# Three gathers in flight instead of five in a product-key retrieval kernel

## The chip, the cores and the metric

The kernel runs on one core of one Trainium2 chip. The metric is the device time of one execution in microseconds; the number quoted for a kernel is the median of several runs. Beside the timed runs there is one profiled execution, from which every view below comes. All arithmetic is 32-bit, on TensorE (PE), VectorE (DVE), ScalarE (ACT) and GpSimd (POOL); SyncE (SP) and ACT issue the direct DMA loads, and POOL issues the indirect ones, which are called gathers here.

## The reference

The input is 256 tokens of width 1024. There are two layers. Each has a mixer (dilated attention and pooling in layer 0, a gated unit in layer 1) and then a channel mixer with product-key retrieval, which is where the change lies:

```python
q = (ht @ w_q).reshape(T, PEER_HEADS, 2, PEER_HALF_DIM)
scores = jnp.einsum('thic,hikc->thik', q, sub_keys)
sv, si = lax.top_k(scores, PEER_TOPK)               # 16 of 128, twice per head
cand = sv[:, :, 0, :, None] + sv[:, :, 1, None, :]
best, ci = lax.top_k(cand.reshape(T, PEER_HEADS, -1), PEER_TOPK)
expert = i1 * PEER_N_KEYS + i2                      # 128 experts per token, of 16384
gate = jax.nn.softmax(best, axis=-1)
hid = jax.nn.gelu(jnp.einsum('cd,ckd->ck', xb, w_down[eb]))
out = jnp.einsum('ck,ckd->cd', gb * hid, w_up[eb])
```

The two expert tables hold 16384 rows of 1024 numbers for each layer.

## The kernel before, in words

**Two ways to the same sum.** The last 160 tokens (DENSE) are handled densely: all 16384 rows of the down table are multiplied with them on TensorE, in 128 blocks of 512 KB, the results are gated with a matrix that is zero where an expert was not picked, and 128 blocks of the up table are multiplied in turn. The first 96 tokens are handled sparsely: their own 128 experts are gathered from memory. One gather brings 128 rows of 4 KB, 512 KB in all, one row to each partition. 96 gathers (ROWS) from the down table serve the 96 tokens of a layer, and 96 more from the up table. For each gathered row VectorE takes one dot product (line 1501, function `dots`, called from `early_dot` in the find stage), or one multiply-add for the up table (line 1618).

**The stages of a layer's channel mixer**, in order of time (layer 0; layer 1 in brackets):

- *The find stage*, about 160 to 337 us (912 to 1092 us). PE multiplies down blocks 0 to 76. Meanwhile DVE finds the picks of tokens 0 to 127 (lines 1466 to 1473 and 1554), after which their gathers can start, then those of tokens 128 to 255. Between the pieces of the second half DVE takes 40 dot products of gathered rows (EARLY = 40), and only then writes the gates of the second half (line 1568). PE must wait for those before it transposes them (lines 1211 and 1214) and goes on with block 77.
- *The one-hot stage*, about 347 to 474 us (1096 to 1225 us). It has 40 passes. In each, PE multiplies one down block and then one set of one-hot matrices (the rows `ps<-oh_buf,ret`). The one-hot matrices of a pass are written half by POOL (two instructions of line 584, function `build_first`), half by DVE and ACT. They have two buffers, so POOL may be two passes ahead of PE.
- *The up stage*, about 474 to 770 us (1223 to 1520 us): 128 up blocks on PE, 96 gathers of the up table.

**What sets the order around the change.** POOL runs its instructions in the order in which they are written. First it issues the first 49 down gathers (`asked = EARLY + RING - 1`). Then, from the fourth of its 40 passes on, it builds the one-hots of a pass and issues the gathers for which a place in the ring will be free. Its gathers write a ring of 10 row buffers of 512 KB. A gather waits for the dot product that last read its buffer (`row_used`), and, if it is a down gather, also for the landing of an earlier gather:

```python
if IN_FLIGHT <= q < ROWS:                                   # line 558
    slot, filled, _ = uses[q - IN_FLIGHT + l * GATHERS]
    pool.wait_ge(row_full[slot], 16 * (filled + 1))
```

While POOL waits there, everything after it on POOL waits as well. The up gathers (q from 96 on) have no such wait.

Down blocks are loaded into 8 buffers, each when PE has used up the block 8 before it. SP issues all of them up to block 39 and from block 80 on; between those SP issues the even ones and ACT the odd ones. Before it issues block 40, SP waits for the gates of the first 128 tokens (line 492).

Of the kernel before, what the change touches and what calls it, by code (L numbers as in the profile page):

```python
# [57 lines left out]
PARTS = P // MORE  # L58
PICKS = RH * TOPK // 2
EXPERTS = KEYS * KEYS  # L60
RING, IN_FLIGHT = 10, 5
UP_RING = 8
DOWN_RAW = 8
ROWS = PICKS + MORE
# [1679 lines left out]
```

## Time and profile before

| | us |
|---|---|
| median of 3 runs (1534.59 to 1537.02) | 1535.36 |
| the profiled execution's own time | 1542.12 |
| its span, first to last instruction | 1540.3 |
| PE busy | 1493.3 (97%) |
| DVE busy | 887.1 (58%) |
| ACT busy | 476.6 (31%) |
| POOL busy | 721.3 (47%) |
| POOL waiting at line 568 for the landing of a down gather | 87.5, 49 times |
| DVE waiting at line 1501 for a gathered row | 24.3, 15 times |

PE is nearly always busy; what it waits for is short and sits between stages. The page's row of GB/s gives the DMA traffic in 40 slices of 38.5 us; it stands near 409 over most of the up stages. "Busy" on POOL at line 568 is the time to write the descriptors of a gather (about 1 us), not the transfer. An idle time in brackets names what ended it.

### The profile page before, as it was taken

The numbers are of one execution on the slowest core, as the hardware profiler recorded it, in microseconds if no ns is written. First come the engines' busy times: TensorE is split into PE (matmuls) and PEld (weight loads), VectorE is DVE, ScalarE is ACT, GpSimd is POOL, SyncE is SP. The second block draws the span as 40 slices with busy tenths as digits, with TensorE's granted clock in tenths as the row PEclk, the third lists the DMA queues.
The fourth block names the chain that finished last, engine by engine and source line by source line (L and its number), as shares of the span: only waits on it lengthen the run. The fifth ranks groups of instructions, "written<-read, shape, count | busy, mean of one in ns | idle before, by whom it ended". The sixth has DMA issues, their size and how long they took to land.

```text
span 1540.3 us, 29722 instructions
## 1 busy us (share of the span) xinstructions
PE 1493.3 (97%) x10668; PEld 1449.4 (94%) x10668; DVE 887.1 (58%) x2900; ACT 476.6 (31%) x1199; POOL 721.3 (47%) x632
## 2 busy tenths in 40 slices
PE   7999999999999999999999999989999999999996
PEld 5789999999999999999977899989999999999996
DVE  1631889856886344443723339998388843444473
ACT  4663331227882000000046542211588600000001
POOL 5568023338996223323457741333599832233250
PEclk9999999999999999999999999999999999999999
DMA  7344899998999999999944468999999999999993
GB/s 276 131 137 165 282 357 406 408 402 314 382 387 392 409 409 410 409 410 410 384 164 161 155 217 301 407 403 409 350 374 378 384 409 409 410 409 410 410 409 135
DMA packets 144992, 523.12 MB, mean 340 GB/s; under 512 B 17008, under 2 KB 17264, under 8 KB 144496
## 3 DMA queue, kind: packets, MB, share of 16 engines
q1 hardware_dynamic: 67696, 240.62, 41.6%
q0 software_dynamic: 55296, 201.35, 33.4%
q10 hardware_dynamic: 21888, 79.70, 13.0%
q8 instruction: 65, 1.06, 0.3%
q14 instruction: 47, 0.39, 0.1%
HBM read 519.48 MB, written 1.05 MB: 338 GB/s over the span
## 4 chain that ended last, share of the span: by engine, by line
PE 78%; DVE 8%; DMA 7%; ACT 3%; issue 2%; POOL 1%; SPq 0%; another core or an unknown queue 0%; DVEq 0%; POOLq 0%; ACTq 0%
PE ps L937 77%; DMA arena<-in_rows,ret 4%; DVE arena L1554 2%; DMA spare<-in_wu 1%; DVE arena L1501 1%; DMA raw<-in_wd 1%; DVE oh_buf L1469 1%; POOL w_lo L551 1%; DVE oh_buf L1466 1%; DVE arena L1473 1%; ACT arena L626 1%; DMA raw<-in_wm 1%; PE ps L945 1%; ACT hT_hi L653 1%; ACT w_hi L638 1%
## 5 line engine op out<-in xcount | busy, mean ns | idle before, releaser
L937 PE MATMUL ps<-arena,raw 128*128 128x160 f32 (+1 forms) x2944 | 416.7, 301 | 4.6 <-DMA raw<-in_wd 4.4
L937 PE MATMUL ps<-arena,w_raw 128*128 128x160 f32 (+1 forms) x2944 | 414.9, 299 | 2.8 <-issue 2.8
L937 PEld LDWEIGHTS ps<-arena,raw 128*128 128x128 f32 x2944 | 407.1, 192 | 6.3 <-DMA raw<-in_wd 4.6
L937 PEld LDWEIGHTS ps<-arena,w_raw 128*128 128x128 f32 x2944 | 403.5, 190 | 4.6 <-issue 4.5
L568 POOL DMA_INDIRECT arena<-in_wu,ret x192 | 190.7, 993 | 362.8 <-DVE oh_buf L1618 272.2
L568 POOL DMA_INDIRECT arena<-in_rows,ret x192 | 202.7, 1056 | 298.3 <-ACT ret L826 104.5
L1618 DVE SCALAR_TENSOR_TENSOR oh_buf<-arena,ret,oh_buf 128x1024 f32<-128x1024 f32 x126 | 161.8, 1284 | 239.1 <-DMA arena<-in_wu,ret 238.9
L551 POOL TENSOR_TENSOR w_lo<-raw,w_hi 128x1024 fp32r<-128x1024 f32 x80 | 193.3, 2424 | 100.7 <-PE ps L937 67.9
L1501 DVE SCALAR_TENSOR_TENSOR arena<-arena,ps 128x1024 f32<-128x1024 f32 x128 | 153.7, 1213 | 0.0
L916 ACT ACTIVATE arena<-ident 128x768 f32<-128x768 f32 x2 | 1.7, 842 | 448.4 <-PE ps L937 448.4
L584 POOL TENSOR_SCALAR oh_buf<-iota,ret 128x128 f32<-128x128 f32 x160 | 127.2, 803 | 15.4 <-PE ps L937 11.3
L804 ACT ACTIVATE arena<-ps 128x160 f32<-128x160 f32 x160 | 48.5, 303 | 276.6 <-PE ps L937 267.0
L937 PE MATMUL ps<-arena 128*128 (+5 forms) x824 | 115.8, 306 | 2.9 <-issue 1.5
L1618 DVE SCALAR_TENSOR_TENSOR ret<-arena,ret 128x1024 f32<-128x1024 f32 x62 | 84.1, 1356 | 57.2 <-DMA arena<-in_wu,ret 54.5
L937 PEld LDWEIGHTS ps<-arena 128*128 128x128 f32 (+2 forms) x824 | 109.7, 190 | 5.8 <-issue 2.5
L638 ACT ACTIVATE w_hi<-raw 128x1024 fp32r<-128x1024 f32 x80 | 83.7, 1060 | 75.6 <-DMA raw<-in_wm 50.6
L849 ACT ACTIVATE ret<-iota,ret 128x128 f32<-128x128 f32 x320 | 100.8, 386 | 4.6 <-PE ps L937 4.6
L1554 DVE SCALAR_TENSOR_TENSOR arena<-iota,ret,ps 128x54 f32<-128x54 f32 x512 | 100.7, 266 | 2.0 <-issue 1.6
L1501 DVE SCALAR_TENSOR_TENSOR arena<-arena,spare 128x1024 f32<-128x1024 f32 x64 | 77.0, 1221 | 24.3 <-DMA arena<-in_rows,ret 24.3
L937 PE MATMUL ps<-arena,spare 128*128 (+1 forms) x576 | 86.6, 300 | 3.4 <-DMA spare<-in_wu 3.3
L937 PE MATMUL ps<-oh_buf,ret 128*128 128x128 f32 x640 | 85.5, 277 | 2.9 <-issue 2.7
L1599 DVE TENSOR_TENSOR arena<-arena,ps 128x512 f32<-128x512 f32 x80 | 54.9, 686 | 56.1 <-PE ps L937 48.6
(144 smaller groups left out, 1779.4 us busy)
## 6 DMA issues: line engine op xcount, KB each, us to landing
raw<-in_wd SPq DMA_DIRECT2D x108, 512.0 KB
w_raw<-in_wd SPq DMA_DIRECT2D x108, 512.0 KB
raw<-in_wm SPq DMA_DIRECT2D x80, 512.0 KB
raw<-in_wu ACTq DMA_DIRECT2D x28, 512.0 KB
raw<-in_wu SPq DMA_DIRECT2D x28, 512.0 KB
w_raw<-in_wu SPq DMA_DIRECT2D x28, 512.0 KB
w_raw<-in_wu ACTq DMA_DIRECT2D x28, 512.0 KB
low_rows<-in_wu SPq DMA_DIRECT2D x22, 512.0 KB
```

The costliest lines, as they stand in the source:

```text
L551: nc.gpsimd.tensor_tensor(w_lo[:, s % WLO, :], raw[:, s, :], whs[:, s].bitcast(F32), ALU.subtract).then_inc(wlo_pool, 1)
L568: nc.gpsimd.indirect_dma_start(ring[s], None, table, bass.IndirectOffsetOnAxis(ap=index, axis=0)).then_inc(row_full[s], 16)
L584: nc.gpsimd.tensor_scalar(oh1g[:, g % 2, k, :], iota[:, :], i1T[:, t:t + 1], gT[:, t:t + 1], ALU.is_equal, ALU.mult).then_inc(oh1_pool, 1)
L626: nc.scalar.activation(junk[:, t, ks], src[:, t, ks], ACT.Square, accum_out=sumsq[:, k, t:t + 1]).then_inc(sumsq_done, 1)
L638: nc.scalar.activation(whs[:, s], raw[:, s, :], ACT.Copy).then_inc(whi_done, 1)
L804: nc.scalar.activation(block_of(b), down_psum(b % SLOTS), ACT.Gelu_apprx_tanh).then_inc(h_done, 1)
L849: nc.scalar.activation(oh2[:, g % 2, k, :], iota[:, :], ACT.Abs, scale=-1.0, bias=i2T[:, t:t + 1]).then_inc(oh2_far, 1)
L937: return nc.tensor.matmul(out, lhsT, rhs, start=start, stop=stop, skip_group_check=shared)
L1501: nc.vector.scalar_tensor_tensor(row, row, 1.0, more_rows if more else h_rows, ALU.mult, ALU.mult, accum_out=(more_hid if more else row_hi ...
L1554: step(nc.vector.scalar_tensor_tensor(found[:, (j * 8 + k) % 24, :], places, cif[:, t, n:n + 1], pay[:, h, :], ALU.is_equal, ALU.mult, acc ...
L1599: nc.vector.tensor_tensor(part, part, gates, ALU.mult).then_inc(gmul_done, 1)
L1618: ins = nc.vector.scalar_tensor_tensor(out, row, coef[:, j:j + 1], out, ALU.mult, ALU.add)
```

## The change

A gather of the down table waits for the landing of the third one before it, in place of the fifth.

```diff
-RING, IN_FLIGHT = 10, 5
+RING, IN_FLIGHT = 10, 3
```

IN_FLIGHT is used only in `gather` (lines 558 and 559). The ring still has 10 buffers, and POOL still asks for as many gathers at each point of its program. No instruction is added, removed or moved on any engine: only the value of 93 waits in each layer is another. The first three gathers of a layer have no such wait now, as the first five had none before.

## Rows read from the trace of the kernel before

**Rows 1.** The page: GB/s in 40 slices; the gathers' queue, packets, MB, share
```profile
GB/s 276 131 137 165 282 357 406 408 402 314 382 387 392 409 409 410 409 410 410 384 164 161 155 217 301 407 403 409 350 374 378 384 409 409 410 409 410 410 409 135
...
q0 software_dynamic: 55296, 201.35, 33.4%
```
**Rows 2.** Chain of waits, layer 0's find stage: start us, us, what
```profile
268.76 16.64 DMA arena<-in_rows,ret
...
319.37 16.29 DMA arena<-in_rows,ret
```
**Rows 3.** PE's timeline: start us, us, engine, line, operation, count [idle before <-releaser]
```profile
308.17 8.86 PE L937 MATMUL ps<-arena,raw 128*128 128x160 f32 x64
...
337.74 0.44 PE L1211 MATMUL ps<-ident,ret 128*128 128x128 f32 x2 [1.15 <-DVE ret L1568]
...
1009.45 11.72 PE L937 MATMUL ps<-arena,raw 128*128 128x160 f32 x64 [4.40 <-DMA raw<-in_wd]
```
**Rows 4.** POOL's timeline, find stages of layer 0 and layer 1
```profile
272.30 0.94 POOL L568 DMA_INDIRECT arena<-in_rows,ret  x1 [2.60 <-DMA arena<-in_rows,ret]
...
334.10 1.30 POOL L568 DMA_INDIRECT arena<-in_rows,ret  x1 [1.73 <-DMA arena<-in_rows,ret]
...
957.17 0.98 POOL L568 DMA_INDIRECT arena<-in_rows,ret  x1 [52.50 <-ACT ret L826]
...
964.36 0.94 POOL L568 DMA_INDIRECT arena<-in_rows,ret  x1 [1.22 <-DMA arena<-in_rows,ret]
...
971.83 0.94 POOL L568 DMA_INDIRECT arena<-in_rows,ret  x1 [1.30 <-DMA arena<-in_rows,ret]
```
**Rows 5.** Busy us of the engines by stretch, granted clock, DMA share, GB/s
```profile
269.00:308.00 39.00, 39.00 (x289) 39.00 (x288) 34.71 (x204) 8.35 (x21) 15.54 (x12) 1.00 1.03 408
385.00:424.00 39.00, 39.00 (x307) 39.00 (x307) 33.79 (x70) 33.21 (x103) 35.43 (x41) 1.00 0.99 381
1010.00:1050.00 40.00, 40.00 (x278) 40.00 (x277) 39.88 (x239) 8.04 (x20) 16.08 (x14) 0.94 1.02 404
```
**Rows 6.** Waits of layer 1, 1060 to 1100 us: us, times, longest
```profile
DVE ret L1572 <- PE ps L1214: 9.1, 1, 9.1
```
**Rows 7.** Chain of waits, layer 1's find stage
```profile
991.15 18.25 DMA raw<-in_wd
```
**Rows 8.** POOL's timeline, layer 0's one-hot stage
```profile
369.24 1.03 POOL L568 DMA_INDIRECT arena<-in_rows,ret  x1 [0.17 <-DVE arena L1501]
370.57 0.94 POOL L568 DMA_INDIRECT arena<-in_rows,ret  x1 [0.30 <-issue]
...
373.31 1.03 POOL L568 DMA_INDIRECT arena<-in_rows,ret  x1 [0.17 <-issue]
...
376.14 1.03 POOL L568 DMA_INDIRECT arena<-in_rows,ret  x1 [0.17 <-issue]
...
378.97 1.03 POOL L568 DMA_INDIRECT arena<-in_rows,ret  x1 [0.16 <-issue]
...
381.80 1.03 POOL L568 DMA_INDIRECT arena<-in_rows,ret  x1 [0.17 <-issue]
383.13 0.94 POOL L568 DMA_INDIRECT arena<-in_rows,ret  x1 [0.30 <-issue]
...
436.12 1.03 POOL L568 DMA_INDIRECT arena<-in_rows,ret  x1 [0.17 <-issue]
...
448.67 1.03 POOL L568 DMA_INDIRECT arena<-in_rows,ret  x1 [0.17 <-DMA arena<-in_rows,ret]
...
463.54 1.59 POOL L584 TENSOR_SCALAR oh_buf<-iota,ret 128x128 f32<-128x128 f32 x2
...
469.20 1.59 POOL L584 TENSOR_SCALAR oh_buf<-iota,ret 128x128 f32<-128x128 f32 x2
```
**Rows 9.** PE's timeline, layer 0's one-hot stage
```profile
465.23 1.13 PE L937 MATMUL ps<-oh_buf,ret 128*128 128x128 f32 x8 [0.29 <-issue]
...
471.44 1.05 PE L937 MATMUL ps<-oh_buf,ret 128*128 128x128 f32 x8
```

## The prediction, made before the changed kernel ran

> **What bounds the kernel now.** I read the page's slices first, then the chain of waits, then the timelines of PE, POOL and DVE at the two places where the chain leaves PE. PE is busy 97% of the span, so a change that adds no work to PE can only act through PE's waits. The slices say that DMA is the second limit. It stands at 406 to 410 GB/s where down blocks and gathers run together, and at 381 to 392 in the middle of the one-hot stages [rows 1]. A gather is 201.35 MB over 384 gathers, 0.524 MB [rows 1], so at 408 GB/s any 512 KB piece, gather or block, costs 1.28 us of all the DMA there is.
>
> The chain leaves PE in layer 0's find stage. From 268.76 to 335.68 us it runs through four landings of gathered rows, about 16 us each, then DVE's last dot products and the gates, and PE waits 1.15 us for these [rows 2, 3]. So layer 0's find stage ends when the 40th row has landed. Layer 1's does not: there DVE has its gates ready and waits 9.1 us for PE [rows 6]. PE itself was late there, because a down block took 18.25 us to land [rows 7]. PE stood for 4.40 us, and the next 64 rows of matmuls took 11.72 us where 64 take 8.86 otherwise [rows 3]; the granted clock over that stretch is 0.94 [rows 5]. That stall therefore cost 4.4 + 2.9 = 7.3 us.
>
> In the one-hot stage PE is busy without a break, but so is POOL. POOL finishes a pass's two one-hots at 463.54 + 1.59 = 465.13, and PE's product of them starts at 465.23 after 0.29 us of idling [rows 8, 9]: PE was waiting for POOL there, whatever name the view gives to the gap. The last pass is ready at 470.79 and used at 471.44, so POOL ends the stage with 0.65 us in hand [rows 8, 9]. A wait put into POOL here is a stall of PE, nearly one for one.
>
> **The one-hot stage, step by step.** 47 down gathers are issued between POOL's passes. The wait for the fifth gather ahead is met nearly always: the idle time before them is a bare 0.16 to 0.30 us [rows 8]. What counts now is the distance to the third one ahead. From the issue times 369.24, 370.57, 373.31, 376.14, 378.97, 381.80, 383.13 [rows 8] the distances are 6.90, 8.40, 8.49 and 6.99 us, and the pattern repeats about every 5 gathers. If a gather lands in less than 6.9 us from its issue, nothing changes. How long does one take? The shortest that the trace shows is the first gather of layer 1, issued at 957.17 and landed before the sixth could start at 964.36: 7.0 us or a little more [rows 4], with others close behind it. The longest inside the stage is the one issued at 436.12, which released the gather at 448.67: 12.4 us [rows 8]. That was with up to five outstanding; with three less queues ahead, and the load at 381 GB/s is below the 408 of the full engine [rows 5]. I take 7.6 us, near the short row. Then each group of five has to be stretched by 7.6 - 6.9 = 0.7 us (one stretch serves the three tight distances, since each spans it), and 47 / 5 = 9.4 groups give 6.6 us, less about 0.6 that POOL has in hand: 6 us for each layer, 12 in all. The ends: 0 below 6.9 us. At 9 us the loose distances tighten as well; every three gathers then take 9 us, so 47 take 141 us, where five take 383.13 - 370.57 = 12.56 us now, and 47 take 118: 23 us in each layer. DVE and ACT have the same buffers to fill and are not the ones late.
>
> **Layer 0's find stage.** From 272.30 to 334.10, over 19 gathers, POOL issued one every 61.8 / 19 = 3.25 us, mostly on the landing of the fifth ahead [rows 4], and each took some 16.3 us [rows 2], which is 5 x 3.27. PE used four down blocks (64 matmul rows) in 8.86 us [rows 3], one every 2.2 us. In GB/s that is 161 for gathers and 237 for blocks, together the 408 of the stretch [rows 5] within 3%. So gathers get what is left by the blocks. With three in flight DMA should stay full, and the time between landings stays 3.25 us, at 9.8 us each. But if the engines serve the two kinds in proportion to what is outstanding, 5 gathers at 161 stand against 7.4 blocks at 237, and 3 gathers against 4.4. Three more blocks have then landed at any moment, and three fewer gathers, though PE has no use for the blocks. The 40th row is late by those three: 3 x 1.28 = 3.9 us if PE's stall leaves all DMA to them, 3 x 3.25 = 9.8 us if not. I take 5 us. A stall of that length brought 2.9 us of slower clock in layer 1, so 8 us. The ends are 0 (DMA does not care how many are outstanding) and 13.
>
> The Trainium skill speaks against this term. Its page "DMA: Bandwidth & Descriptors", section "Queues, rings and completion order", says that each DMA engine takes turns between the queues that have work, a packet at a time. By that rule the share of the gathers would not depend on how many are outstanding so long as there are some, and this term would be 0. The trace doesn't decide it.
>
> **Layer 1's find stage.** Fewer gathers ahead of the late block should shorten its 18.25 us: two of 0.524 MB are 2.6 us, and the 4.4 us stall with its clock loss could go altogether, up to 7.3 us gained. DVE's lead of 9.1 us [rows 6] is larger than that. But the same lateness of the rows as in layer 0, 4 to 10 us, eats the lead: PE comes 7.3 us earlier and finds the gates 9.1 - 4 = 5 us early or 9.1 - 10 = 1 us late. I take 0 for the sum of the two, with ends -7 and +6.
>
> **The up stage.** Its gathers have no such wait, its DMA stands at 409 GB/s [rows 1] and its length is not touched. What the down stages lose is not given back, since only 16 buffers of up blocks can be filled ahead.
>
> **The sum.** 8 + 0 + 12 = 20 us. The profiled execution took 1542.12 us, span 1540.3, and would take 1562; its own time is 6.8 us above the median of the runs. The median of 1535.4 goes to 1555 us.
>
> **The rivals.**
>
> *Queues take turns.* The depth does not change any share of the DMA. Then layer 0's find stage costs 0, layer 1 gains some of its stall, say 4 us, and the one-hot stage still pays 12: 1535.4 + 8 = 1543 us. For it: in layer 0 gathers got exactly what blocks left over, which turn-taking explains as well. Against it: at the start of layer 1's gathers the sixth to the tenth were issued on four landings between 964.36 and 971.83 [rows 4], one in 1.87 us or 280 GB/s, more than an even turn with the blocks would give.
>
> *Blocks come first, and the gathers land soon enough.* The mechanism is the late block of layer 1, and the price is its stall with the clock, 7.3 us. It decides if a gather lands in under 6.9 us in the one-hot stage, so that POOL never waits, and if the 40th row of layer 0 is less than 1 us later. Then the kernel is at 1535.4 - 6 = 1529 us. For it: three in flight should cut the latency, and the rule about turns supports the rest. Against it: 7.0 us is the shortest landing in the rows, already above 6.9.
>
> *POOL pays in full.* The landing stays at 9 us in the one-hot stage because down blocks of both queues and the gathers keep the engines at 0.99 busy [rows 5]. 23 x 2 + 8 = 54 us: 1589 us. For it: the 12.4 us row. Against it: with POOL slower the load falls, and the latency with it.
>
> *Nothing happens.* The landing is at the edge, gain and loss cancel: 1535 us. POOL's 49 waits for a landing just get another name.
>
> **How the numbers follow.** The forecast of about 1555 has 0.45, turns 0.20, POOL in full 0.12, blocks first 0.14, nothing 0.09. Changes under 0.2% (3 us) can't be told from none for this kernel. Slower: 0.45 + 0.20 + 0.12, less a little for the edge of the second, 0.76. Faster: 0.15. Same: 0.09. The range has to reach from the faster case's upper edge, 1531, to beyond the likeliest one's high side (8 us of landing, 10 us in each layer, and 13 in the find stage: 1569) and close to POOL in full: 1531 to 1588. The likeliest case alone spans 1543 to 1570.
>
> **What would show it.** In the one-hot stage, line 568 of POOL should show waits for landings of 0.3 to 1 us at about three of five gathers, and PE should show gaps at the products from oh_buf, summing to some 6 us in each layer. In layer 0's find stage PE's wait at line 1211 should be 4 to 10 us in place of 1.15, with the landings near 10 us and a gather every 3.3 us. In layer 1 the stall at 1009 us should be shorter and DVE's 9.1 us wait should shrink. The forecast is wrong if the one-hot stages keep their length, which would mean that landings take under 6.9 us, or if gathers come further apart than 3.3 us in the find stage, which would mean that three do not keep DMA full.

## The result, and where the time went

The changed kernel takes 1576.53 us (median of 4, 1574.87 to 1578.53) against 1536.19 us for the kernel before in the same comparison. The ratio is 1.0247, with a 95% interval of 1.023 to 1.0263: about 38 us, or 2.5%, slower (the medians are 40 us apart). The forecast was 20 us. The measured time lies inside the stated range, but the loss is twice the forecast.

The change also adds two waits to each layer, for the fourth and the fifth gather; the other 91 have another value.

The two profiled executions are 1542.12 and 1574.87 us, 32.7 us apart. The one of before took longer than any of the timed runs and the one of after is the fastest of its own, so the stages below add up to 32.7 and not to 38.

The page's slices answer to those of [rows 1], and the group of POOL's gathers shows the new waits:

```profile
GB/s 278 121 148 183 289 360 407 381 355 332 361 351 371 409 409 410 410 410 409 346 194 155 159 221 333 406 397 402 266 350 348 334 407 408 409 410 409 410 409 139
...
L568 POOL DMA_INDIRECT arena<-in_rows,ret x192 | 201.7, 1051 | 341.9 <-DMA arena<-in_rows,ret 186.9
```

Slices 8 to 13 of the 40 stand at 332 to 381 where they stood at 314 to 408, and the up stages at 409 to 410 as before. POOL waits 186.9 us for landings of down gathers where it waited 87.5.

PE's timeline in the changed kernel (start us, us, engine, line, operation, idle before and what ended it) answers to [rows 3, 9]:

```profile
342.32 0.69 PE L1211 MATMUL ps<-ident,ret 128*128 128x128 f32 x2 [9.94 <-DVE ret L1568]
355.12 1.13 PE L937 MATMUL ps<-oh_buf,ret 128*128 128x128 f32 x8 [1.07 <-ACT ret L857]
...
483.48 1.05 PE L937 MATMUL ps<-oh_buf,ret 128*128 128x128 f32 x8
...
1106.02 0.69 PE L1211 MATMUL ps<-ident,ret 128*128 128x128 f32 x2 [9.95 <-DVE ret L1568]
1106.92 9.08 PE L937 MATMUL ps<-arena,w_raw 128*128 128x160 f32 x48
...
1121.85 1.87 PE L937 MATMUL ps<-oh_buf,ret 128*128 128x128 f32 x8 [3.67 <-issue]
...
1223.10 1.13 PE L937 MATMUL ps<-oh_buf,ret 128*128 128x128 f32 x8 [1.85 <-ACT ret L857]
...
1254.62 1.05 PE L937 MATMUL ps<-oh_buf,ret 128*128 128x128 f32 x8
```

PE waits almost 10 us for the gates in both layers. In layer 1 the stall on a late down block is gone (no idle of PE between 990 and 1096 us). These starts, with the first gather of each layer (205.00 and 957.17 us before, 204.35 and 968.88 after), cut the span into stages. "Find" runs from a layer's first gather to PE's row of line 1211, "handover" from there to PE's first product of one-hots, "one-hot" from that product to the last one.

| stage | before | after | more |
|---|---|---|---|
| to the first gather, layer 0 | 205.00 | 204.35 | -0.65 |
| find, layer 0 | 132.74 | 137.97 | 5.23 |
| handover, layer 0 | 11.52 | 12.80 | 1.28 |
| one-hot, layer 0 | 122.18 | 128.36 | 6.18 |
| up stage, and layer 1 to its first gather | 485.73 | 485.40 | -0.33 |
| find, layer 1 | 135.55 | 137.14 | 1.59 |
| handover, layer 1 | 9.14 | 15.83 | 6.69 |
| one-hot, layer 1 | 120.45 | 132.77 | 12.32 |
| the rest | 317.99 | 318.38 | 0.39 |

The sum is 32.7 us. The one-hot stages have 18.5 of it, the find stages with their handovers 14.8, and the up stages have neither paid nor won. The kernel with the seventh gather ahead (experiment 4) takes the same time as before, and its profiled execution (1537.09 us) is nearer to the median. Against that one the same cuts give 37.7 us: 20.9 in the one-hot stages, 7.0 in find and handover of layer 0, 9.8 in those of layer 1. The layer 1 starts of before come from its own timeline:

```profile
1092.72 0.38 PE L1211 MATMUL ps<-ident,ret 128*128 128x128 f32 x2
...
1101.86 1.05 PE L937 MATMUL ps<-oh_buf,ret 128*128 128x128 f32 x8
...
1222.31 1.05 PE L937 MATMUL ps<-oh_buf,ret 128*128 128x128 f32 x8
```

In the one-hot stage POOL's timeline of the changed kernel (layer 1) answers to [rows 8]:

```profile
1173.44 1.03 POOL L568 DMA_INDIRECT arena<-in_rows,ret  x1 [0.17 <-DMA arena<-in_rows,ret]
...
1176.27 1.03 POOL L568 DMA_INDIRECT arena<-in_rows,ret  x1 [0.17 <-issue]
...
1179.10 1.03 POOL L568 DMA_INDIRECT arena<-in_rows,ret  x1 [0.17 <-issue]
1182.01 0.94 POOL L568 DMA_INDIRECT arena<-in_rows,ret  x1 [1.88 <-DMA arena<-in_rows,ret]
1182.99 1.59 POOL L584 TENSOR_SCALAR oh_buf<-iota,ret 128x128 f32<-128x128 f32 x2
...
1187.57 1.03 POOL L568 DMA_INDIRECT arena<-in_rows,ret  x1 [0.17 <-DMA arena<-in_rows,ret]
...
1196.34 0.94 POOL L568 DMA_INDIRECT arena<-in_rows,ret  x1 [2.08 <-DMA arena<-in_rows,ret]
```

Where a gather waits, it is the second of a pass with two. In all, 5 gathers of layer 0's one-hot stage and 7 of layer 1's wait longer than 0.3 us, 7.6 and 11.9 us together, and PE stands for 6.5 and 8.3 us. The third ahead was issued at 1173.44 and releases it at 1182.01, 8.6 us later; the next time it is 8.8 us (1187.57 to 1196.34). Over all such waits of this kernel and of experiment 2 it is 7.8 to 9.8 us, mostly 8 to 9. The idle time is 1.88 and 2.08 us, POOL's one-hots of the next pass come later by that, and PE shows a gap of some 1.8 us, as at 1223.10, once the lead is spent.

### The profile page after: what moved, and what is told of

Read it like the earlier page. It is cut to its first block, busy times and chain, and to the rows that moved or that the text cites. A ratio compares the mean times of both kernels' runs of the same rounds, so it can differ in the third digit from the quotient of the medians.

```text
span 1573.0 us, 29724 instructions
## 1 busy us (share of the span) xinstructions
PE 1497.2 (95%) x10668; PEld 1452.7 (92%) x10668; DVE 887.8 (56%) x2900; ACT 478.1 (30%) x1199; POOL 716.9 (46%) x632
## 3 DMA queue, kind: packets, MB, share of 16 engines
HBM read 519.48 MB, written 1.05 MB: 331 GB/s over the span
## 4 chain that ended last, share of the span: by engine, by line
PE 50%; DMA 30%; DVE 9%; issue 5%; ACT 4%; POOL 2%; SPq 0%; DVEq 0%; POOLq 0%; ACTq 0%
PE ps L937 49%; DMA arena<-in_wu,ret 15%; DMA arena<-in_rows,ret 14%; DVE arena L1554 2%; DVE ret L1618 1%; POOL w_lo L551 1%; DVE arena L1501 1%; DVE oh_buf L1469 1%; DMA spare<-in_wu 1%; ACT arena L626 1%; PE ps L945 1%; DVE oh_buf L1466 1%; DMA raw<-in_wm 1%; ACT hT_hi L653 1%; DVE oh_buf L1618 1%
## 5 line engine op out<-in xcount | busy, mean ns | idle before, releaser
L937 PEld LDWEIGHTS ps<-arena,w_raw 128*128 128x128 f32 x2944 | 409.3, 192 | 0.0
L568 POOL DMA_INDIRECT arena<-in_rows,ret x192 | 201.7, 1051 | 341.9 <-DMA arena<-in_rows,ret 186.9
L568 POOL DMA_INDIRECT arena<-in_wu,ret x192 | 187.5, 976 | 364.3 <-DVE oh_buf L1618 280.9
L638 ACT ACTIVATE w_hi<-raw 128x1024 fp32r<-128x1024 f32 x80 | 83.7, 1060 | 74.4 <-DMA raw<-in_wm 53.3
L937 PE MATMUL ps<-oh_buf,ret 128*128 128x128 f32 x640 | 86.3, 278 | 19.6 <-ACT ret L857 10.4
L937 PEld LDWEIGHTS ps<-oh_buf,ret 128*128 128x128 f32 x640 | 79.9, 193 | 23.2 <-ACT ret L857 11.7
```

The source lines that it names most:

```text
L568: nc.gpsimd.indirect_dma_start(ring[s], None, table, bass.IndirectOffsetOnAxis(ap=index, axis=0)).then_inc(row_full[s], 16)
L638: nc.scalar.activation(whs[:, s], raw[:, s, :], ACT.Copy).then_inc(whi_done, 1)
L937: return nc.tensor.matmul(out, lhsT, rhs, start=start, stop=stop, skip_group_check=shared)
```

## The experiments

Each was compared with the kernel before on its own chip. "Find", "handover" and "one-hot" are taken from the profiled execution of each as above, in us, layer 0 / layer 1. That is one execution for each kernel, and differences of 2 to 4 us between single entries can't be told from scatter:

| kernel | ratio to before (95%) | find | handover | one-hot |
|---|---|---|---|---|
| before | 1 | 132.7 / 135.6 | 11.5 / 9.1 | 122.2 / 120.5 |
| third ahead (the change) | 1.0247 (1.023 to 1.0263) | 138.0 / 137.1 | 12.8 / 15.8 | 128.4 / 132.8 |
| 1. third in the find stage only | 1.0122 (1.0082 to 1.0161) | 137.2 / 135.9 | 13.5 / 13.2 | 121.9 / 121.9 |
| 2. third in the one-hot stage only | 1.0138 (1.0112 to 1.0164) | 133.7 / 133.0 | 9.1 / 9.1 | 130.3 / 131.3 |
| 3. fourth | 1.0041 (1.0018 to 1.0064) | 134.4 / 133.5 | 9.1 / 11.2 | 120.1 / 120.2 |
| 4. seventh | 1.0000 (0.9988 to 1.0011) | 134.6 / 134.0 | 9.1 / 9.1 | 120.1 / 120.1 |
| 5. as 1, down blocks loaded later | 1.0160 (1.0145 to 1.0176) | 135.9 / 133.3 | 12.8 / 16.6 | 122.2 / 122.5 |
| 6. as 1, last five gathers free | 1.0056 (1.0035 to 1.0076) | 133.2 / 135.2 | 10.9 / 10.7 | 120.2 / 120.1 |
| 7. fifth, SP's wait later | 1.0015 (1.0005 to 1.0025) | 133.1 / 134.1 | 10.9 / 10.7 | 120.1 / 120.2 |
| 8. fourth, SP's wait later | 1.0028 (1.0018 to 1.0038) | 134.4 / 134.6 | 10.9 / 11.4 | 120.5 / 120.8 |

**1 and 2. The change in one stage alone.**

```diff
-                    if IN_FLIGHT <= q < ROWS:
-                        slot, filled, _ = uses[q - IN_FLIGHT + l * GATHERS]
+                    if (3 if q < EARLY + RING - 1 else 5) <= q < ROWS:
+                        slot, filled, _ = uses[q - (3 if q < EARLY + RING - 1 else 5) + l * GATHERS]
```

The second has 5 and 3 the other way round. Expected of the first:

> Only the first 49 gathers of a layer (those issued before the one-hot passes) wait for the third ahead; the rest wait for the fifth again. Theory A (the traces of before and after, stage by stage): the find stages with the handover to the one-hots cost 6.5 us in layer 0 and 13.1 us in layer 1, the one-hot stages 6.2 and 7.5 us, and the two add up. Then this kernel is 19.6 us slower than before, about 1556 us, the wait of PE at line 1211 stays near 9.9 us in both layers, and the one-hot stages take 122.2 us from first to last product as before. Rival B (most of the loss lies in the one-hot stages, and the late start of these is only where it begins to show): 6 us slower or less, about 1542 us.

Expected of the second:

> The reverse: the first 49 gathers wait for the fifth ahead as before, those between the one-hot passes for the third. Theory A: 6.2 + 7.5 = 13.7 us slower, about 1550 us, find stages as before (PE's wait at line 1211 about 1 us, the late down block of layer 1 there again), POOL waiting 1.4 to 2 us for a landing once in about five gathers. Rival B: 25 us or more slower. Rival C (the waits of POOL come from a backlog that the find stage leaves behind): nearly no loss, under 3 us.

Measured: 1553.44 and 1555.06 us against 1534.27, so 1.22% or 19 us, and 1.38% or 21 us. Together that is 2.60%, and the whole change costs 2.47%: the halves add up, and rival B is out from both sides. Rival C is out too, since the one-hot stages grow to 130.3 and 131.3 us with find stages as before. The texts on record split layer 1's loss wrongly: they reckoned its one-hot stage from the second product. From the first it is 12.3 us and not 7.5, so the 19.6 us expected of experiment 1 become 14.8, and the 13.7 of experiment 2 become 18.5; 19 and 21 were measured. Against the profile of experiment 4, which leaves out what was slow in the profiled execution of before, the whole change has 16.8 and 20.9 us in these two parts.

PE's waits at line 1211 in experiment 1 are 9.48 and 8.73 us, near the 9.9 expected. POOL's gathers and one-hots in experiment 1, layer 0, show what comes after that wait:

```profile
340.48 1.30 POOL L568 DMA_INDIRECT arena<-in_rows,ret  x1 [1.50 <-DMA arena<-in_rows,ret]
...
343.33 0.94 POOL L568 DMA_INDIRECT arena<-in_rows,ret  x1 [0.31 <-issue]
345.85 0.94 POOL L568 DMA_INDIRECT arena<-in_rows,ret  x1 [1.58 <-DMA arena<-in_rows,ret]
...
352.62 0.94 POOL L568 DMA_INDIRECT arena<-in_rows,ret  x1 [2.33 <-DMA arena<-in_rows,ret]
353.61 4.70 POOL L584 TENSOR_SCALAR oh_buf<-iota,ret 128x128 f32<-128x128 f32 x6
```

DVE takes the 40th row at 339.75, and the landing of that row is what lets the gather at 340.48, number 43, go. So POOL still owes seven gathers before its first one-hot. It ends them at 353.6; before, it was done at 347.6.

**3 and 4. Other depths.** The edit is `RING, IN_FLIGHT = 10, 4` and `10, 7`.

> The fourth ahead everywhere. In the one-hot stage the distance to the fourth gather ahead is at least 9.7 us, against landings of about 8.5 us that the waits of the changed kernel imply, so the one-hot stages should cost 0 to 2 us each. In the find stages theory A has DMA full again (401 GB/s and more where three in flight gave 391 and 394) and about one down block fewer ahead than with three, so about 3 us in layer 0 and about 6 in layer 1. Sum: about 10 us slower, 1546 us. Rival D (a latency limit: three can't cover the landing time, four can): within 3 us of before.

> The seventh ahead everywhere. Theory A (rows and down blocks share one full DMA): rows of the find stage come earlier, down blocks later. PE's 1.15 us wait of layer 0 goes, and the late down block of layer 1 comes later by up to 2 x 1.28 = 2.6 us, so its stall grows from 4.4 to about 7 us; layer 1 has 9.1 us of slack on the side of the rows, so that loss counts in full. Sum: about 2 us slower, 1534 to 1541 us. Rival E (more in flight is better throughout): 3 us or more faster.

Measured: 1539.89 us (0.41% slower, 6 us) for four, and 1535.06 against 1534.27, no difference, for seven. With four the one-hot stages are at 120.1 and 120.2 us, which is 39 passes at PE's own pace of 3.07. The distance to the fourth ahead (9.7 us and more) is above what nearly all landings take that POOL waits for (7.8 to 9.8 us, mostly 8 to 9), and the distance to the third is not. That fixes the mechanism of that half. In the find stages four shows no loss against five in its profile, so theory A was too high there and rival D too low in the time; where the 6 us of the median are, its profile (1536.5 us, below its median) does not show. For seven, theory A said 2 us slower, and the interval allows 1.7; rival E is out. In its profile PE's wait of layer 0 is gone, and PE stands 4.7 us in each layer for late blocks, as A had it.

The DMA rate in a stretch of layer 0's find stage (busy us of PE, PEld, DVE, ACT, POOL; granted clock, DMA share, GB/s), for the kernel before, then experiment 1, then experiment 3, then experiment 6, which has three in flight up to gather 44:

```profile
269.00:335.00 66.00, 66.00 (x488) 66.00 (x487) 52.75 (x307) 12.30 (x34) 25.39 (x20) 1.00 1.03 407
```
```profile
269.00:335.00 66.00, 63.32 (x467) 63.08 (x465) 45.26 (x263) 11.66 (x32) 24.19 (x20) 1.00 1.01 392
```
```profile
269.00:335.00 66.00, 66.00 (x488) 66.00 (x488) 49.16 (x273) 12.21 (x34) 24.78 (x20) 1.00 1.02 402
```
```profile
269.00:335.00 66.00, 66.00 (x488) 66.00 (x487) 47.63 (x268) 11.98 (x33) 24.95 (x20) 1.00 1.02 401
```

Here five in flight stand at 407, four at 402, three at 392 or 401. PE's idle end of the second stretch is not the reason for the 392: in the changed kernel 269 to 308 us, with PE busy throughout, stood at 390. What differs in experiment 6 is that PE had stood 1.89 us for a late down block at 253.63. So three in flight can leave the DMA less than full, and did so in the two executions in which PE had not been late. That the eight block buffers are then full, so that few blocks are outstanding, would explain it, but isn't shown.

**5. Down blocks loaded two blocks later.** As experiment 1, and:

```diff
-                    sp.wait_ge(w_used, l * LAYER + MIX_BLOCKS + b - DOWN_RAW + 1)
+                    sp.wait_ge(w_used, l * LAYER + MIX_BLOCKS + b - DOWN_RAW + 3)
...
-                    if MORE_GATES_AT <= n < ALONE_FROM and n % 2:
+                    m = n - 2
+                    if MORE_GATES_AT <= m < ALONE_FROM and m % 2:
```

(ACT then loads block m in place of n.)

> As the kernel in which only the first 49 gathers wait for the third ahead (18.7 us slower than before), but each down block is loaded two blocks later, when PE has used up the block 6 before it in place of 8. Theory A (down blocks that run ahead take the DMA time of the rows): up to two blocks fewer have landed when row 40 is due, so PE's wait at line 1211 shrinks by up to 2 x 1.28 = 2.6 us in each layer from 9.5 and 8.7, and the kernel comes to about 1549 us. Rival F (three gathers in flight are limited by their own round trip, since DMA stood at 390 to 394 GB/s and not 408): the wait stays at 9 us or grows and DMA is still less full, 1553 us or more. A late down block with a stall of PE would show that 6 buffers are too few and add to either.

The time, 1559.67 us or 1.6% slower, is on F's side, but the mechanism is A's. The rows did come earlier when fewer blocks ran ahead. DVE's gates (line 1568, here 1569) were written 128.2 us after the first gather in layer 0 and 130.8 in layer 1, against 136.9 and 135.6 in experiment 1. PE's 9 us waits were gone, and DMA stood at 401 GB/s from 269 to 335 us. But now PE stalled on down blocks (line numbers are one higher in this kernel):

```profile
252.82 2.44 PE L938 MATMUL ps<-arena,w_raw 128*128 128x160 f32 x16 [0.99 <-DMA w_raw<-in_wd]
258.22 10.63 PE L938 MATMUL ps<-arena,raw 128*128 128x160 f32 x64 [2.96 <-DMA raw<-in_wd]
...
340.41 0.38 PE L1212 MATMUL ps<-ident,ret 128*128 128x128 f32 x2
...
353.24 1.43 PE L938 MATMUL ps<-oh_buf,ret 128*128 128x128 f32 x8 [3.54 <-issue]
...
512.89 3.27 PE L938 MATMUL ps<-arena,spare 128*128 128x160 f32 x16 [3.44 <-DMA spare<-in_wu]
```

So rows and blocks trade places in one pipe. Counted by queue over the first 127 us of the find stage, the DMA moved 50.0 and 49.9 MB here against 50.1 and 50.4 in experiment 1, but the gathers got 21.4 and 20.9 MB of it in place of 19.8 and 20.0, and the blocks 28.4 and 28.8 in place of 30.1 and 30.3.

The find stage became 1.3 and 2.6 us shorter than in experiment 1 and the kernel no faster, because PE's wait for the gates was not the only thing late. POOL's first one-hot comes after its 49th gather, and that one was issued 146.1 and 147.2 us after the first, in experiment 1 148.0 and 146.5, before 141.6 and 138.1:

```profile
350.56 0.94 POOL L568 DMA_INDIRECT arena<-in_rows,ret  x1 [2.70 <-DMA arena<-in_rows,ret]
351.55 4.80 POOL L584 TENSOR_SCALAR oh_buf<-iota,ret 128x128 f32<-128x128 f32 x6
```

PE's first product follows POOL's first one-hot by 1.7 us, in both experiments and both layers, so find and handover together are 148.8 and 149.8 us here against 150.7 and 149.1. The other 5.7 us that this kernel takes more than experiment 1 between layer 0's last one-hot product and layer 1's first gather are mostly the wait for a late up block at 512.89 (3.44 us, and 16 rows in 3.27 us after it); experiment 1 has no such wait there. Why that block is late isn't shown. So the time on F's side is no evidence for F.

**6. The last five of the 49 gathers free.**

```diff
-                    if IN_FLIGHT <= q < ROWS:
-                        slot, filled, _ = uses[q - IN_FLIGHT + l * GATHERS]
+                    if (3 if q < EARLY + 4 else 10 if q < EARLY + RING - 1 else 5) <= q < ROWS:
+                        slot, filled, _ = uses[q - (3 if q < EARLY + 4 else 10 if q < EARLY + RING - 1 else 5) + l * GATHERS]
```

> The first 44 gathers of a layer wait for the third ahead, numbers 45 to 49 for none, the others for the fifth. This leaves the landing of row 40 nearly where it was and takes away only the time that POOL stands at the last five before its first one-hot. Theory A: that handover costs PE about 2.2 us in each layer (the gap before its first product from oh_buf), so this kernel is 4 us faster than the one with all of the first 49 on the third, about 1549 us, and the gap is gone. Rival G: PE's gap has another cause (its slower clock after the 9 us wait, DVE or ACT) and stays; 1553 us.

Measured: 1542.87 us, 0.56% slower than before where experiment 1 was 1.22%. That is 10 us won against experiment 1 where 4 were expected, with intervals of 0.4% and 0.2% to either side on the two. In the profile the handovers are 10.9 and 10.7 us in place of 13.5 and 13.2, 5.1 us in all, and POOL starts its one-hots at 346.92 in place of 353.61. Rival G is out: layer 1 has no gap, and the 1.57 us of layer 0 end with ACT, not with POOL. In this one execution the one-hot stages are also 1.7 us shorter each, and layer 0's find stage 4.0 us, which five gathers issued after the 40th row has landed can't bring. So 5 us of the 10 are seen in the handovers; the two intervals allow the rest as scatter. The find stage of layer 0 shows that scatter: with three in flight as in experiment 1, PE here stood 1.89 us for a late block at 253.63, the gates came 132.9 us after the first gather in place of 136.9, and PE waited only 1.70 us for them. In layer 1, where PE was never late, it waited 8.04.

**7 and 8. SP's wait behind four more down blocks**, to win what three in flight had won in layer 1:

```diff
+                blocks(sp, load_down_even, MORE_GATES_AT, MORE_GATES_AT + DOWN_RAW, DOWN_RAW)
                 sp.wait_ge(idg_done, TILES * l + 1)
...
-                blocks(sp, load_down_even, MORE_GATES_AT, ALONE_FROM, DOWN_RAW)
+                blocks(sp, load_down_even, MORE_GATES_AT + DOWN_RAW, ALONE_FROM, DOWN_RAW)
```

> The kernel before (fifth ahead), except that SP issues down blocks 40, 42, 44 and 46 before it waits for the first half's gates, and copies the gates after them. Theory H: the late down block of layer 1 (18.25 us to land, 4.4 us of stall and 2.9 us of slower clock) is block 40, held up by that wait, and it is what three in flight had cured. Then the stall is gone at the fifth ahead too, and PE gains up to 7 us in layer 1, less what the rows lack of slack (5.5 to 9.1 us): 4 to 7 us faster, about 1529 us. Rival I: the block is late because five gathers fill the DMA, whoever issues it when; then the stall stays and the time is within 2 us of before.

> The same with the fourth ahead in place of the fifth. Four kept the one-hot stages at their length (120.1 and 120.2 us) and had 7.7 us of slack at line 1211 in layer 0. Theory H: also 4 to 7 us faster than before, about 1530 us. Rival I: within 0.4% above before, as four was without this edit.

Measured: 1.0015 and 1.0028, slightly slower, and both theories failed. PE's timeline with the fifth ahead (line numbers again one higher):

```profile
1000.66 8.96 PE L938 MATMUL ps<-arena,raw 128*128 128x160 f32 x64 [1.05 <-DMA raw<-in_wd]
...
1086.16 0.69 PE L1212 MATMUL ps<-ident,ret 128*128 128x128 f32 x2 [4.82 <-DVE ret L1569]
```

The stall shrank from 4.40 to 1.05 us, and its slower clock went (64 rows in 8.96 us, not 11.72), as H said and I denied. But PE now waits 4.82 us for the rows in place of the 9.1 us that DVE waited for PE, and the find stage is 134.1 us. No version tried here beats the kernel before.

## Why the prediction was wrong

The forecast was 8 us in layer 0's find stage, 0 in layer 1's and 12 in the one-hot stages. Measured between the two profiles are 6.5, 8.3 and 18.5 us, or 7.0, 9.8 and 20.9 against the profile of experiment 4. Two terms failed: layer 1's 0, where PE's wait was counted from the wrong arrival and the handover was left out, and the one-hot stages' 12, where the landing was taken too short.

**The one-hot stages: right mechanism, mis-sized.** The forecast put the price into the distance to the third gather ahead (6.9 to 8.5 us) against the time of a landing, with POOL as the engine without slack. Experiments 2 and 3 show that. The step that failed is the landing: the term was 6 us in each layer, from a landing of 7.6 us, and the landings that POOL waited for took 8 to 9. Measured in the changed kernel were 6.2 and 12.3 us, and 21 us in both layers together in experiment 2. By the prediction's rule, (8.7 - 6.9) x 9.4 - 0.6 would be 16 us in each layer, so the rule is too high with the right landing: it has each of the 9.4 groups wait, and in the four one-hot stages of the changed kernel and experiment 2 only 5 to 8 gathers waited. The sign given was 0.3 to 1 us at three gathers of five; it was 0.8 to 2.3 us at one of six to nine. 7.6 us had been taken as "near the short row", the first gather of a stage with none ahead of it [rows 4]. That row shows the best case, and the stage's own row had 12.4 us.

**Layer 0's find stage: right in size, by two causes and some luck.** Forecast were 8 us with the clock, and a wait of 4 to 10 us at line 1211 in place of 1.15. The wait is 9.94 us, and find and handover together are 6.5 us longer. Of the wait, 5.2 us are later gates and 3.6 are a PE that came earlier, which no term had. Both causes weighed for the later gates are there. Over the first 127 us of the stage the gathers got 19.8 MB in place of 21.8; of these 2.0 MB, 0.9 went to blocks, which ran ahead, and the rest was not moved at all (393 GB/s in place of 402). The prediction had taken DMA to stay full and named the sign against it, gathers more than 3.3 us apart: from the 20th to the 40th they came every 3.6 us in place of 3.3. Experiment 5 gives the blocks' part back to the rows. That the size fits is partly luck, since experiment 6, also with three in flight there, shows a wait of 1.70 us.

**Layer 1's find stage and handover: the step that failed.** The prediction set gain and loss against each other and took 0, with ends of -7 and +6. They are 1.6 + 6.7 = 8.3 us longer, beyond the upper end. The gain came (PE had no stall and stood at the gates 8.4 us earlier, counted from the first gather), but the gates were written 136.8 us after the first gather in place of 126.9, 9.9 us later. That is the upper end of the 4 to 10 us forecast, ate all of the 9.1 us of slack [rows 6], and leaves the find stage 1.6 us longer, near the "1 us late" of the prediction. What failed is what was made of it. The prediction counted the gates from PE's old arrival (9.1 - 4 and 9.1 - 10). Counted from a PE that comes 7.3 us earlier, the same numbers give a wait of 2 to 8 us at the gates, and 9.95 was measured. Such a wait costs clock in layer 0's term but not in this one, and 2.4 us of it came. The rest of the 6.7 us is the handover, below, at which the term put nothing.

Why the gates' lateness came out at its upper end: a PE that no longer stalls uses and asks for more blocks, and these take DMA time from the rows. The queues over the first 127 us of the stage show it (q0 is the gathers', q1 and q10 carry the blocks; packets, MB, share of 16 engines), before and then after:

```profile
q0 software_dynamic: 6244, 22.78, 45.8%
q1 hardware_dynamic: 5126, 18.00, 35.8%
q10 hardware_dynamic: 2730, 9.95, 19.7%
```
```profile
q0 software_dynamic: 5461, 19.90, 40.4%
q1 hardware_dynamic: 5609, 19.76, 39.6%
q10 hardware_dynamic: 2880, 10.49, 20.9%
```

The gathers lost 2.9 MB, 5.5 of them, and the blocks took 2.3 of it; the rest is the lower rate (396 GB/s, not 401). Experiment 7 tells the two apart roughly: with five in flight and a stall of only 1.05 us the gates came at 133.8. So about 7 of the 9.9 us come with the missing stall, and about 3 with the depth.

**The handover: not in the prediction at all.** Nine gathers stand between the 40th row and POOL's first one-hot. With the rows late and at most three in flight these end late too: the 49th is issued 148.1 and 150.3 us after the first, in place of 141.6 and 138.1. PE comes out of its 10 us wait with a slower clock (48 rows in 9.08 us, at a granted clock of 0.50, the 1.2 GHz level, from 1106 to 1110.5 us and 0.73 over all of them; before, they took 6.69 at 1.00, 2.4 GHz), still finds no one-hots, and idles 3.67 us in layer 1. Of layer 1's 6.7 us, 2.4 are this clock and 3.7 the wait for POOL. Two chains end here within a few us of each other, the gates with PE's blocks and POOL's 49 gathers. Experiment 5 shortened the first and gained nothing; experiment 6 shortened the second and took the handover from 13.4 to 10.8 us.

**The rivals.** "Queues take turns" would have left layer 0's find stage as it was; it grew by 5.2 us. That rule of the Trainium skill ("DMA: Bandwidth & Descriptors", "Queues, rings and completion order") doesn't exclude it, since it speaks of queues that have work, and whether the gathers' queue on one engine was at times without work no view here shows: they give sums over 16 engines. From 269 to 308 us before, these sums are 1722 packets for the gathers and 1341 and 1294 for the two queues of blocks. Equal turns of three queues that always have work would give equal counts. "Blocks first" failed at its own condition, a landing under 6.9 us. "POOL pays in full" named 9 us of landing and 23 us for each layer: the landing was nearly right, but experiment 2 paid 10.5 us for each: the loose distances never tightened, and 7 and 8 gathers waited, 10.9 and 12.0 us in all.

## What to carry to other kernels

Between POOL's passes here, a limit on transfers in flight cost nothing until the distance between an issue and the one it waits for fell below the landing time under load. Take that time from the busiest stretch of the stage itself, not from the first transfer of a burst. Where a queue is in order, list everything that stands between the late landing and the engine's next work for others, here nine gathers before the first one-hot. And where two streams share a DMA that is nearly full, a stall taken from one consumer can come back as the wait of the other, so count the bytes of each due before the meeting point before adding up stalls.

## What the runs showed that was not expected

- Whichever side waits, the find stage ends at nearly the same time: 132.7 to 135.6 us over all kernels with four or more in flight, in both layers, with PE's stalls on late blocks between 0 and 4.7 us and its wait for the rows between 0 and 6.3.
- Four in flight are enough for the one-hot stage and three are not: 120.1 and 120.2 us against 130.3 and 131.3.
- Beside the stream of down blocks, from 269 to 335 us, five gathers of 0.524 MB in flight went with 407 GB/s, four with 402, and three with 392 or, in experiments 5 and 6, 401.
- Waiting for the gates is not the same as losing time: in experiment 5 PE's 9 us waits were gone, and the first product of one-hots came no more than 1.9 us earlier, since POOL's 49th gather was nearly as late.
